# Token rows of an expert picked and transposed in one product, in a fused layer with a mixture of experts

## The reference, cut to what matters

```python
logits = h @ router_w + router_b              # 256 tokens, 32 experts
top_logit, top_idx = lax.top_k(logits, 4)
gates = softmax(top_logit)
for each expert e, for the tokens that chose it:
    xb  = h[tokens of e]                      # token rows, gathered
    gu  = xb @ moe_w_gu[e] + moe_b_gu[e]      # 1024 x 2048 weights
    glu = minimum(gu[:, :1024], 7.0)
    lin = clip(gu[:, 1024:], -7.0, 7.0)
    act = glu * sigmoid(1.702 * glu) * (lin + 1.0)
    y[tokens of e] += gate * (act @ moe_w_down[e] + moe_b_down[e])
```

## Time and profile before

| | us |
|---|---|
| median of 3 runs | 1302.47 |
| lowest and highest | 1298.92, 1303.51 |
| the profiled execution's own time | 1299.72 |
| its span | 1298.0 |
| TensorE busy with products | 1182.1 (91%) |
| TensorE loading weights | 475.2 (37%) |
| VectorE busy | 313.2 |
| ScalarE busy | 228.2 |

### The profile page before, as it was taken

One profiled execution on the slowest core, in us unless ns is written; L12 is line 12 of the kernel. 1 busy time (PEld: TensorE's weight loads), 2 busy tenths in 40 slices (PEclk: granted clock), 3 DMA queues, 4 the chain that ended last, 5 costly groups with the idle time before them and its releaser, 6 DMA issues.

```text
span 1298.0 us, 17311 instructions
## 1 busy us (share of the span) xinstructions
PE 1182.1 (91%) x7132; PEld 475.2 (37%) x7132; DVE 313.2 (24%) x632; ACT 228.2 (18%) x381; POOL 39.4 (3%) x70
## 2 busy tenths in 40 slices
PE   4989998887999999999999999999999999999994
PEld 1435587663433333333333333332333333333231
DVE  1204567643212111111211111111121111111113
ACT  2112255523111111111111111111111111111112
POOL 0300100000000000000000000000000000000000
PEclk9999999998899999999999999999999999999997
DMA  9898001069099999999999999999999999999991
GB/s 373 285 372 342 6 3 61 17 246 406 26 426 429 428 428 428 428 428 428 427 427 428 428 428 427 428 428 428 426 429 428 428 427 428 428 428 428 428 428 57
DMA packets 44241, 459.94 MB, mean 354 GB/s; under 512 B 5112, under 2 KB 7328, under 8 KB 16432
## 3 DMA queue, kind: packets, MB, share of 16 engines
q1 hardware_dynamic: 41152, 451.98, 82.9%
q0 software_dynamic: 2576, 6.35, 1.7%
q10 hardware_dynamic: 480, 1.13, 0.2%
HBM read 457.96 MB, written 1.47 MB: 354 GB/s over the span
## 4 chain that ended last, share of the span: by engine, by line
DMA 53%; PE 39%; DVE 4%; ACT 2%; issue 1%; DVEq 0%; SPq 0%; ACTq 0%
DMA ring<-in_moe_w_gu_dram 47%; PE bank L1177 16%; PE bank L575 5%; PE bank L1197 4%; DMA ring<-in_w_mod_dram 3%; DMA ring<-in_w_in_dram 1%; DMA proj<-in_norm_ffn_g_dram 1%; PE bank L689 1%; PE bank L550 1%; PE bank L1140 1%; PE bank L1155 1%; PE bank L563 1%; PE bank L1167 1%; PE bank L1099 1%; DMA const_sb<-in_constants_dram 1%
## 5 line engine op out<-in xcount | busy, mean ns | idle before, releaser
L1177 PE MATMUL bank<-ring,proj 128*64 128x512 f32 x2048 | 459.6, 599 | 32.9 <-DMA ring<-in_moe_w_gu_dram 32.6
L1177 PEld LDWEIGHTS bank<-ring,proj 128*64 128x64 f32 x2048 | 140.6, 137 | 350.4 <-issue 275.8
L1197 PE MATMUL bank<-ring,proj 128*64 128x512 f32 x1024 | 233.8, 598 | 11.9 <-DVE proj L2073 11.9
L2064 DVE TENSOR_SCALAR proj<-bank 128x512 f32<-128x512 f32 x32 | 22.1, 692 | 481.3 <-PE bank L1177 481.3
L1540 ACT ACTIVATE proj<-proj 128x512 f32<-128x512 f32 x32 | 20.2, 630 | 605.1 <-DVE proj L2064 605.1
L1197 PEld LDWEIGHTS bank<-ring,proj 128*64 128x64 f32 x1024 | 69.0, 136 | 131.9 <-issue 131.9
L575 PE MATMUL bank<-ring,hT 128*128 128x512 f32 (+2 forms) x224 | 88.6, 551 | 0.2 <-DMA ring<-in_w_in_dram 0.2
L2076 DVE COPY proj<-bank 128x512 f32<-128x512 f32 x32 | 22.1, 691 | 249.1 <-PE bank L1197 249.1
L1155 PE MATMUL bank<-proj 64*128 64x512 f32 x256 | 63.6, 615 | 0.0
L1140 PE MATMUL bank<-h_nat,proj 128*64 128x512 f32 x264 | 62.3, 593 | 0.0
L575 PEld LDWEIGHTS bank<-ring,hT 128*128 128x128 f32 x224 | 41.7, 190 | 44.7 <-issue 39.0
(11 more groups left out here) (332 smaller groups left out, 793.5 us busy)
## 6 DMA issues: line engine op xcount, KB each, us to landing
ring<-in_moe_w_gu_dram SPq DMA_DIRECT2D x128, 2048.0 KB, 24.4
ring<-in_moe_w_down_dram SPq DMA_DIRECT2D x64, 2048.0 KB, 21.7
ring<-in_w_mod_dram SPq DMA_DIRECT2D x12, 2048.0 KB, 15.6
ring<-in_w_in_dram SPq DMA_DIRECT2D x5, 2048.0 KB, 17.3
ring<-in_w_out_dram SPq DMA_DIRECT2D x2, 2048.0 KB, 8.4
const_sb<-in_constants_dram POOLq DMA_DIRECT2D x1, 2450.0 KB, 13.0
ring<-in_w_in_dram SPq DMA_DIRECT2D x1, 1536.0 KB, 9.6
ring<-in_w_in_dram SPq DMA_DIRECT2D x1, 1024.0 KB, 13.6
```

Source lines behind the costliest of these rows:

```text
L1177: mm = pe.matmul(b[CAP * half:CAP * half + CAP, :], xT[:, k % 4, k // 4, :], ring[:, j, 2048 * kc + o + 512 * half:2048 * kc + o + 512 * h ...
L1197: mm = pe.matmul(b_down[CAP * half:CAP * half + CAP, :], aT[:, k % 4, k // 4, :], ring[:, 4 + j, D * kc + 512 * half:D * kc + 512 * half + ...
L2064: ts(moe["glu"], bank[4][:, :], LIMIT, None, ALU.min).then_inc(sem("glu_sb"), 1)
```

## The change

The gathered rows are no longer formed and then transposed. The token rows themselves are now the weights, and the one-hot matrix is streamed: `h`, taken in columns four elements apart, gives 128 features by 64 places at once, already transposed. It takes 16 products of 64 columns in place of 4 products of 512, and writes bank 7 in the layout that `turn` gave. The transposes of `xe` go, and with them ScalarE's copy of `xe` and the semaphores `xe_sb` and `xeT_full`. The wait for `xeT_sb` moves behind the products of the biases.

```diff
@@ -1135,11 +1135,13 @@
 
             def gather():
 
-                for s in range(2):
+                cols = h_t[:, :].rearrange("p (s h k c) -> p s h c k", s=2, h=2, c=4)
+                for c in range(4):
                     for half in range(2):
-                        mm = pe.matmul(b_misc[CAP * half:CAP * half + CAP, :], moe["hot"][:, CAP * s:CAP * s + CAP],
-                                       h[:, s, 512 * half:512 * half + 512], start=(s == 0), stop=(s == 1),
-                                       skip_group_check=True)
+                        o = CAP * (2 * c + half)
+                        for s in range(2):
+                            mm = pe.matmul(b_misc[:, o:o + CAP], cols[:, s, half, c, :], moe["hot"][:, CAP * s:CAP * s + CAP],
+                                           start=(o == 0 and s == 0), stop=(s == 1), skip_group_check=True)
                 mm.then_inc(sem("xe_full"), 1)
 
             def turn(out, src):
@@ -1160,7 +1162,6 @@
 
                 xT = moe["xeT"].rearrange("p (c h m) -> p c h m", c=4, h=2)
                 aT = moe["actT"].rearrange("p (c h m) -> p c h m", c=4, h=2)
-                pe.wait_ge(sem("xeT_sb"), n + 1)
                 pe.wait_ge(sem("bias_gu"), 16 * (n + 1))
                 for q, b in enumerate((b_glu, b_glu, b_lin, b_lin)):
                     half = q % 2
@@ -1168,6 +1169,7 @@
                                    param[32 * q:32 * q + 1, 3 * D:3 * D + 512],
                                    start=True, stop=False, skip_group_check=True)
                 mm.then_inc(sem("bias_used"), 1)
+                pe.wait_ge(sem("xeT_sb"), n + 1)
                 for j in range(4):
                     pe.wait_ge(ring_full[j], 16 * (n + 1) + 16 * FRONT_ROUNDS[j])
                     for kc in range(2):
@@ -1186,8 +1188,6 @@
                 scatter()
                 pe.wait_ge(sem("act_ready"), n + 1)
                 turn(b_down, moe["act"]).then_inc(sem("actT_full"), 1)
-                pe.wait_ge(sem("xe_sb"), n + 2)
-                turn(b_misc, moe["xe"]).then_inc(sem("xeT_full"), 1)
                 pe.wait_ge(sem("actT_sb"), n + 1)
                 for j in range(2):
                     pe.wait_ge(ring_full[4 + j], 16 * (n + 1) + 16 * FRONT_ROUNDS[4 + j])
@@ -1214,8 +1214,6 @@
                 for half in range(2):
                     pe.matmul(acc[2 * s + half][:, :], gate_t[:, P * s:P * s + P], b_down_sb[:, 512 * half:512 * half + 512],
                               start=True, stop=False, skip_group_check=True)
-            pe.wait_ge(sem("xe_sb"), 1)
-            turn(b_misc, moe["xe"]).then_inc(sem("xeT_full"), 1)
             with pe.Fori(0, NE) as e:
                 expert(e)
             need = pe.value_load(count_i[0:1, 0:1])
@@ -1529,23 +1527,17 @@
 
             def gathered(n):
                 act.wait_ge(sem("xe_full"), n)
-                A(moe["xe"], bank[7][:, :], ACT.Copy).then_inc(sem("xe_sb"), 1)
-
-            def turned(n):
-                act.wait_ge(sem("xeT_full"), n)
                 A(moe["xeT"], bank[7][:, :], ACT.Copy).then_inc(sem("xeT_sb"), 1)
 
             def expert(n):
                 act.wait_ge(sem("glu_sb"), n + 1)
                 A(moe["sig"], moe["glu"], ACT.Sigmoid, scale=ALPHA).then_inc(sem("sig_sb"), 1)
                 gathered(n + 2)
-                turned(n + 2)
                 act.wait_ge(sem("scat_full"), n + 1)
                 act.wait_ge(sem("scattered"), n + 1)
                 A(moe["scat"], bank[7][:, 0:2 * P], ACT.Copy).then_inc(sem("scat_sb"), 1)
 
             gathered(1)
-            turned(1)
             with act.Fori(0, NE) as e:
                 expert(e)
             need = act.value_load(count_i[0:1, 0:1])
```

## The result

The changed kernel takes 1522.14 us (median of 6 runs, 1520.35 to 1523.77) against 1299.96 us for the kernel before on the same chips: a ratio of 1.170, 95% interval 1.1685 to 1.1719. The forecast was slower, 1333 us and at most 1378; the loss is more than six times the 33.6 us forecast. The profiled execution took 1520.35 us with a span of 1518.7.

A forecast was written before the change was run, and what follows sets the result against it. Transfers (29.52 us a round) were taken to bound most rounds, TensorE some seven; TensorE at 30.04 would then bound all 31, +29.7 us, with +2.4 tail and +1.5 prologue +33.6 on 1299.7: 1333 us, range 1316 to 1378.

The forecast's parts named there:

- What bounds the kernel before: Expert loop: transfers need 29.52 us a round, TensorE's own work 27.68, so about 1.84 us a round is spare.
- What leaves: Each expert round: four transposes, a ScalarE copy and two semaphore hops go, biases' products move ahead; all costed at nothing.
- What comes: Gather in each round: 32 records at about 0.122 us, 4.17 us in place of 1.81, +2.36 us.
- the router's extra 2 ns: Gather's record distance: router's contiguous loads at 0.112 us against 0.110 for contiguous transposes, added to the strided transposes' 0.120.
- The upper bound: Gather: strided loads not overlapping at all, 0.213 us a record, 6.90 us, +5.09 a round, 1421 us.
- rival 1: Gather: strided loads cost more than in eight transposes; 0.16 us a record gives 1368 us, 0.213 gives 1421; 15%.
- two rows 10 us apart: Gather's price per record: 0.120 us from strided transposes or 0.112 from contiguous loads, about 10 us of the total.
- rival 3: Expert rounds: clock falls, one half-clock stretch per round costs 2.5 us, 78 in all, about 1410 us; 5%.
- Rival 4: Gather: the step does not matter beside 64 columns, 0.112 us a record, round 29.74, 1323.5 us; 13%.
- The prologue and the tail: Ahead of the loop +1.5 us, between -0.5 and +3.7; last gather on the chain to the end +2.4 us.

The follow-up runs named there:

- e3: Kernel before without the second four transposes, one ScalarE copy and two semaphore hops, the experts multiplying untransposed tokens: 1296.38 us, ratio 0.9977.
- e2: Kernel before with only the wait for the transposed tokens moved behind the biases' products: 1296.83 us, ratio 0.9982.
- e4: Kernel before with short runs of f32 products and transposes at various weight steps and widths added, to price each record: one execution, 1315.92 us.
- e7: Changed kernel with right values and contiguous gather weights, VectorE sorting h's features once ahead of the loop: 1325.86 us, ratio 1.0200.
- e5: Changed kernel, strided loads kept, but each gather product streams 128 columns in place of 64 (values wrong): 1450.65 us, ratio 1.1153.
- e1: Changed kernel with the gather's weights in contiguous columns instead of every fourth, features in another order: 1325.48 us, ratio 1.0194.
- e6: Changed kernel with a step of two elements between the gather's weight columns instead of four: 1331.79 us, ratio 1.0243.

## Why the prediction was wrong

- **What bounds the kernel before**: right. TensorE's spare time was 1.84 us a round, and the waits for transfers are gone after the change, as said. The rounds are not equal, though, as was forecast: the clock spreads them from 34.77 to 37.46 us. e3 shows that shedding TensorE work buys nothing in a round.
- **What leaves** (transposes, copy, hops at nothing; biases at nothing): right, e3 and e2.
- **What comes**: this is the step that failed. "I take the strided distance with the router's extra 2 ns: 0.122 us" borrowed the distance of the strided transposes for products. e4 has both on the same weights: 0.121 for the transpose, 0.235 for the product. The term was +2.36 us a round, with 0.10 in it for the change to full-array products, and is +5.95 with the same 0.10, which is 31x3.59 = 111 us. The upper bound was there: loads that do not overlap, 0.213 us a record and 1421 us, and it too was low, since a load of 0.212 was itself a transpose's, where the gather's loads last 329 ns. I gave it 15% and let the range end at 1378. (The sums of rival 1 and of this bound also leave out the 0.10, 3 us of the total.)
- **"Advanced Engine Details and Errata", section "SBUF Cachelines"**, in the Trainium skill, says 16-byte lines and a penalty for each access to another one. The runs agree, and give the penalty: 1.83 ns a line in f32 product loads. For transposes there is one strided step alone (0.121 at a step of 4, 0.109 at 1), so that at most 0.95 ns a line can be said. I used the page to choose between two rows 10 us apart; the step was worth 197. The other rule, columns/1.2 ns from the Trainium skill's "TensorE: Matmul & The Clock Gate", section "LDWEIGHTS (loading the stationary operand)", gives 107 ns and holds nearly for contiguous columns at the full clock (0.11), not for a step of four (0.235), and not for contiguous columns at half clock (6.99/32 = 0.218 in e7).
- **The clock** was rival 3, 5% and as an alternative to the others. It came on top: 2.09 us a round, 64.8 us (the 67.9 of the table less the 0.10 of each round), and e5 shows that it hung on how little the array streamed beside the slow loads. With contiguous columns (e1) and a step of two (e6) the granted clock is 1.00 in the rounds. So slower loads left the array idler, and rival 1 made rival 3 likelier: I had listed them as if only one could come. The reason that I gave against it, slices that mostly show 9, says little: in the rounds of the changed kernel they show 8 or 9 too, over a mean granted clock of 0.89.
- **Rival 4**, the contiguous price, was 1323.5 us with a round of 29.74; e1 has 1325.5 and 29.68. So the way from a record's distance to the time was sound, and with 0.235 in it the same sum gives a period of 27.68+31x0.235+0.10+0.30-1.81 = 33.56, which e5 has as 33.63.
- **The prologue and the tail**, +1.5 and +2.4, measured +5.0 and +9.8, both longer by the same gather and by half clock around it (slot 4's products at 1489.26 take 5.32 us in place of 3.65). The 3.5 and 7.4 us that these two were off by, the 111 of the gather and the 65 of the clock are the 187 us between the forecast of 1333 and the profiled 1520.35.

## What to carry to other kernels

Price a strided f32 weight load by the 16-byte lines that it touches and by the kind of record that it belongs to; a row of a transpose is no price for an f32 product, here it was half. Where many weights must be picked at a step, sort them once by a copy, so that the loads are contiguous. When a new stretch leaves the array waiting for loads, count the clock as part of its price: the products behind it may pay more than the stretch itself suggests.

## What the hardware showed that was not expected

- The distance of short f32 products is proportional to the lines touched by their weights (0.119, 0.175, 0.235 us for 64, 96, 128 lines), stops rising at one line per column (0.238 at a step of 8), and with 128 lines is the same at half clock. That of contiguous weights is not: the same gather takes 3.71 us at the full clock and 6.99 at half.
- A transpose with the same strided weights takes half of it, 0.121 us. An f32 product has two records where a transpose has one, and each of the two pays double. Why was not tried.
- More columns streamed beside slow loads made the kernel 71.5 us faster, since the granted clock stayed at 1.00 in place of 0.89 (the mean over the rounds).
